# Final norm with tokens on partitions behind the eighth expert, and router logits from the un-normalised stream

## The chip, the core and the metric

The kernel runs on one core of one Trainium2 chip. The core has engines that run side by side and meet at semaphores: TensorE (PE, with PEld for its weight loads), VectorE (DVE), ScalarE (ACT), GpSimd (POOL) and SyncE (SP), which here issues every DMA. Each engine has a sequencer that works through its own list of instructions, branches included. The metric is the device time of one execution in microseconds (us); lower is better. A profiled execution also has a span, from the first to the last record of the program.

## The reference

A trunk of two layers over 256 tokens of 1024 features. Each layer adds a gated mixer, a cross-attention and a channel mixer to the stream h. In layer 1 the channel mixer is a mixture of 8 experts, of which each token takes two, and a norm ends the whole:

```python
def rms_norm(x, g):
    x32 = x.astype(jnp.float32)
    y = x32 * lax.rsqrt(jnp.mean(x32 * x32, axis=-1, keepdims=True) + EPS)
    return (y * g.astype(jnp.float32)).astype(x.dtype)

def moe_swiglu(xn, router_w, w1, w3, w2):
    ...
    logits = (xt @ router_w).astype(jnp.float32)
    top_v, top_e = lax.top_k(logits, TOP_K)
    gate = jax.nn.softmax(top_v, axis=-1)
    ...
    def expert_block(args):
        xblk, e = args
        return (jax.nn.silu(xblk @ w1[e]) * (xblk @ w3[e])) @ w2[e]
    ...

        hn = rms_norm(h, norm_ffn_g[l])
        ...
            h = h + moe_swiglu(hn, router_w[j], moe_w1[j], moe_w3[j], moe_w2[j])
    return rms_norm(h, final_norm_g)
```

The second choice's logit less the first's decides the gates; the order of a token's logits does not change when all of them are multiplied by the token's 1/rms.

## The kernel before

**Layout.** The stream `h` lies with features on partitions: 8 blocks of 128 features by 256 tokens (`h[:, k, :]`). Weights come from HBM in chunks of 1 MB (`raw`, 128x2048). For each chunk ACT writes a rounded copy `w_hi`, DVE the rest `w_lo`, and PE forms each product from three fp32r matmuls (`three`, L1519 to L1521), so that it keeps fp32's accuracy. Each engine's list is written out by hand; nothing reorders it. ACT and DVE split a chunk three steps ahead of the one whose results they post-process.

**Layer 1 up to the experts.** The last four chunks are the attention's output projection (`xo`, chunks `XO0` to `XO0 + 3`, 48 matmuls each). Behind each, DVE adds the result to a quarter of the stream (`residual`, L1143) and signals `h_att`; ACT squares that quarter into `cacc` (`square`, L673), and PE sums the squares over features with a matrix of ones (`sum_squares`, L1566), two chunks later. When all four are summed, ACT takes the root (L677), DVE the reciprocal (L1033), then DVE multiplies the stream by the gain and 1/rms into `xf` (L1040), while ACT and DVE split `xf` into `b_hi` and `b_lo`. From `xf` PE forms the 8 logits of each token (L1802, 16 fp32 matmuls) and turns it so that tokens lie on partitions (`by_token`, L1810); ACT copies that to `h_tok`. DVE finds each token's two experts (`route`, L1435 to L1459), with an exponential on ACT (L988) for the gates, and PE counts ranks within experts (L1819). `select` (L1374) makes a 0/1 matrix of the tokens of an expert, and the gather (L1829) multiplies `h_tok` by it. DVE then keeps books of further blocks (`further_blocks`, L1464 to L1486), which exist when an expert has more than 128 tokens.

**The experts.** A loop of 8 passes (L1919 for PE, `e_block`) has 42 chunks in each. At the end of a pass ACT and DVE write the expert's gated result to `y_hi_e` and `y_lo_e` (L973, L1416), tokens' slots on partitions. Within the next pass PE spreads it back to the tokens (`spread_out`, L1901 and L1902) and DVE adds it to `h` (L1389). The gather for the next expert also stands in the pass (L1913).

**The end.** Each engine then reads the number of blocks (`value_load`, L1922 for PE, L554 for SP) and runs a second loop of 3 passes (L1923, L555), each under an `If` (L1924, L556) around a whole further block. Then PE, ACT and DVE drain and meet at `settled`. Only now is the last expert spread and added to `h` (L1506), squared (L1003), summed (L1933), its root taken (L1005), the reciprocal formed (L1508), the norm applied (L1510) and turned (L1810), copied by ACT (L1008) and stored in two DMAs (L560).

## Time and profile before

| | us |
|---|---|
| median of 3 runs | 2162.11 |
| lowest, highest | 2160.7, 2167.48 |
| profiled execution | 2162.14 |
| its span | 2160.3 |
| PE busy | 2059.6 |
| DVE busy | 1637.2 |
| ACT busy | 1299.9 |

A timeline row tells when an instruction (or a run of like ones, with x and their number) started, how long it took, its engine, line, operation and tiles, and in brackets how long its engine had been idle and what ended that. An fp32 matmul stands as two records, an fp32r matmul or a transpose as one. Engines with a q (PEldq, SPq) are the sequencers. A window row has for each engine the busy time and the number of instructions, then the granted clock of PE as a share of full speed and the DMA's share.

### The profile page before, as it was taken

Reading aid. Unit: us, or ns where it says so; the run is one execution under the profiler, and the core shown is the slowest. Engines: PE = TensorE matmul, PEld = TensorE weight load, DVE = VectorE, ACT = ScalarE, POOL = GpSimd, SP = SyncE. Lnnn points to the kernel's source line nnn. Section 1 sums busy time; section 2 is a strip of 40 time slices with the busy share of each in tenths; the row PEclk is TensorE's granted clock in tenths of the full one; section 3 lists DMA queues with packets and bytes.
Section 4 is the critical chain, followed back from the end, with each engine's and each line's share of the span. In section 5 each row is a group of like instructions: output and inputs, shape, how many; then the busy total and the mean of one; then the engine's idle time right before and its main releaser. Section 6 shows DMA issues by size and latency. Waiting matters only on the chain.

```text
span 2160.3 us, 33554 instructions
## 1 busy us (share of the span) xinstructions
PE 2059.6 (95%) x12929; PEld 1871.5 (87%) x12929; DVE 1637.2 (76%) x1704; ACT 1299.9 (60%) x1133; POOL 13.2 (1%) x71
## 2 busy tenths in 40 slices
PE   8998999999998998989979999999999999999996
PEld 8988989889998988989878888888888888888885
DVE  6988656554446888656559888888988888898885
ACT  6664354343334664454337777777777777777774
POOL 0000000000000000000000000000000000000000
PEclk9998999999999999999989999999999999999998
DMA  8544445435554545445437999999999999999892
GB/s 248 176 124 161 132 155 176 151 117 181 190 176 145 167 124 161 135 152 175 139 136 285 385 325 376 330 366 353 354 373 331 376 332 367 343 366 373 328 377 91
DMA packets 309518, 526.76 MB, mean 244 GB/s; under 512 B 13566, under 2 KB 156582, under 8 KB 309414
## 3 DMA queue, kind: packets, MB, share of 16 engines
q1 hardware_dynamic: 309414, 525.29, 69.7%
q8 instruction: 75, 1.23, 0.2%
q14 instruction: 29, 0.24, 0.0%
HBM read 524.21 MB, written 1.05 MB: 243 GB/s over the span
## 4 chain that ended last, share of the span: by engine, by line
PE 80%; DVE 9%; issue 4%; ACT 4%; SPq 1%; PEldq 0%; DMA 0%; PEld 0%; DVEq 0%; ACTq 0%; POOL 0%
PE ps L1519 25%; PE ps L1521 24%; PE ps L1520 24%; DVE w_lo L1017 2%; DVE c L1083 2%; ACT w_hi L662 2%; PE ps L1839 1%; ACT w_hi L669 1%; PE ps L1913 1%; PE ps L1634 1%; DVE cacc L1067 1%; PE ps L1566 1%; PE ps L1654 1%; PE ps L1901 0%; PE ps L1902 0%
## 5 line engine op out<-in xcount | busy, mean ns | idle before, releaser
L1017 DVE TENSOR_TENSOR w_lo<-raw,w_hi 128x2048 fp32r<-128x2048 f32 x330 | 752.5, 2281 | 368.4 <-ACT w_hi L662 304.4
L1519 PE MATMUL ps<-w_hi,a_hi 128*128 128x512 f32 (+1 forms) x1472 | 566.1, 385 | 0.6 <-DVE h L1389 0.4
L1521 PE MATMUL ps<-w_hi,a_lo 128*128 128x512 f32 (+1 forms) x1472 | 560.5, 381 | 0.0
L1520 PE MATMUL ps<-w_lo,a_hi 128*128 128x512 f32 (+1 forms) x1472 | 559.7, 380 | 0.0
L662 ACT ACTIVATE w_hi<-raw 128x2048 fp32r<-128x2048 f32 x159 | 301.4, 1896 | 292.0 <-PE ps L1521 284.2
L1519 PE MATMUL ps<-a_hi,w_hi 128*128 128x256 f32 x1520 | 442.2, 291 | 24.1 <-DVE a_lo L1017 16.2
L1520 PE MATMUL ps<-a_lo,w_hi 128*128 128x256 f32 x1520 | 436.6, 287 | 0.0
L1521 PE MATMUL ps<-a_hi,w_lo 128*128 128x256 f32 x1520 | 436.1, 287 | 0.0
L669 ACT ACTIVATE w_hi<-raw 128x2048 fp32r<-128x2048 f32 x171 | 328.0, 1918 | 123.4 <-PE ps L1521 123.4
L1521 PEld LDWEIGHTS ps<-w_hi,a_lo 128*128 128x128 f32 x1472 | 276.5, 188 | 53.6
L1519 PEld LDWEIGHTS ps<-w_hi,a_hi 128*128 128x128 f32 x1472 | 276.7, 188 | 51.5 <-DVE w_lo L1017 0.8
L1519 PEld LDWEIGHTS ps<-a_hi,w_hi 128*128 128x128 f32 x1520 | 298.5, 196 | 26.3 <-issue 17.8
L1520 PEld LDWEIGHTS ps<-w_lo,a_hi 128*128 128x128 f32 x1472 | 276.8, 188 | 50.6
L1520 PEld LDWEIGHTS ps<-a_lo,w_hi 128*128 128x128 f32 x1520 | 298.4, 196 | 0.5
L1521 PEld LDWEIGHTS ps<-a_hi,w_lo 128*128 128x128 f32 x1520 | 298.0, 196 | 0.0
L1519 PE MATMUL ps<-b_hi,w_hi 128*128 128x256 f32 x744 | 214.3, 288 | 15.8 <-DVE b_lo L1017 14.7
L1521 PE MATMUL ps<-b_hi,w_lo 128*128 128x256 f32 x744 | 212.3, 285 | 0.0
L1520 PE MATMUL ps<-b_lo,w_hi 128*128 128x256 f32 x744 | 212.3, 285 | 0.0
L1519 PEld LDWEIGHTS ps<-b_hi,w_hi 128*128 128x128 f32 x744 | 144.6, 194 | 17.6 <-DVE b_lo L1017 10.7
L1017 DVE TENSOR_TENSOR w_lo<-mem_t,w_hi 128x2048 fp32r<-128x2048 f32 x56 | 128.4, 2292 | 21.7 <-ACT w_hi L669 21.6
L1520 PEld LDWEIGHTS ps<-b_lo,w_hi 128*128 128x128 f32 x744 | 144.6, 194 | 0.2
L1521 PEld LDWEIGHTS ps<-b_hi,w_lo 128*128 128x128 f32 x744 | 144.6, 194 | 0.0
(284 smaller groups left out, 2169.9 us busy)
## 6 DMA issues: line engine op xcount, KB each, us to landing
raw<-in_moe_w SPq DMA_DIRECT2D x171, 1024.0 KB, 6.6
raw<-in_w_in SPq DMA_DIRECT2D x68, 1024.0 KB, 5.2
mem_t<-in_moe_w SPq DMA_DIRECT2D x56, 1024.0 KB, 6.4
area<-in_moe_w SPq DMA_DIRECT2D x56, 1024.0 KB, 6.3
xf<-in_moe_w SPq DMA_DIRECT2D x56, 1024.0 KB, 6.0
raw<-in_ffn_w SPq DMA_DIRECT2D x33, 1024.0 KB, 5.3
raw<-in_w_mlstm_out SPq DMA_DIRECT2D x8, 1024.0 KB, 5.0
raw<-in_w_out SPq DMA_DIRECT2D x8, 1024.0 KB, 5.0
```

What stands on the lines that cost most here:

```text
L662: act.activation(w_hi[c % SPL][:, 0:n], raw[c % RAW][:, 0:n], ACT.Copy).then_inc(hi_done.sem, 1)
L669: act.activation(w_hi[m % SPL][:, :], e_raw[m % ERAW][:, 0:CH], ACT.Copy).then_inc(e_hi.sem, 1)
L1017: return dve.tensor_tensor(dst, whole, as_f32(hi), ALU.subtract)
L1067: ins = dve.scalar_tensor_tensor(dst, src, tap, dst, ALU.mult, ALU.add)
L1083: ins = dve.scalar_tensor_tensor(dst, src, tap, dst, ALU.mult, ALU.add)
L1519: pe.matmul(dst, wh, xh, start=start, stop=False, skip_group_check=True)
L1520: pe.matmul(dst, wh, xl, start=False, stop=False, skip_group_check=True)
L1521: return pe.matmul(dst, wl, xh, start=False, stop=stop, skip_group_check=True)
L1566: ins = pe.matmul(ps[4][:, 0:T], ones[:, :], sq[:, j % 2, i * T:(i + 1) * T], start=(j == 0 and i == 0), stop=(j == 3 and i == 1), skip_gr ...
L1634: ins = pe.matmul(ps[4 + hd % 2][:, tt * T:(tt + 1) * T], q_t[:, k, tt * P:(tt + 1) * P], k_t[:, k, :], start=(tt == 0 and e == 0), stop=( ...
L1654: ins = pe.matmul(ps[7][:, e * T:(e + 1) * T], vx[:, m, hd, e * P:(e + 1) * P], z_sig[:, 4 + 2 * (hd % 2) + m, :], start=(e == 0 and m == ...
L1839: ins = pe.transpose(ps[6][:, k * P:(k + 1) * P], act_e[g % 2][:, k * P:(k + 1) * P], ident[:, :])
```

## The change

**The logits.** The weights of the router are loaded behind the load of chunk `WO0` and multiplied by the norm's gain on DVE (8 instructions behind chunk `XK0`). In layer 1 `router_pair` takes the place of `sum_squares` for the last norm, one chunk behind the addition and no longer two: it forms logits from `h` itself (4 matmuls) and sums the squares for tokens on partitions (4 matmuls with one column of ones). ACT writes `xf = h * gain` by pairs behind its squares. The norm on features (`norm(layer, 2, ...)`) is made in layer 0 only. 1/rms is a column of one number per token, `r_stat[1]`; it scales `h_tok` in ACT's copy, and the difference of the two best logits. The order of `route` changes: ranks and `select(0)` stand ahead of the gates, which get a semaphore of their own (`gate_ready`). The three zeroing instructions (`sel_t`, `y_hi_e`, `y_lo_e`) move from the start of `route` to the first `xo` step. The split of chunk 2 of the first expert moves behind the routing on ACT and behind `gather_lo(0)` on DVE. `further_blocks` works on tables that lie side by side, with three instructions in a row where it had seven each.

**The final norm.** `tail(b)` stands on PE, ACT and DVE directly behind the loop of 8, ahead of the loop over further blocks (and inside its `If`, for a further block). PE turns `h` into four banks by products with the identity and adds the last expert's result into the same banks, with tokens on partitions. ACT squares the banks with a sum along the row; DVE and ACT form 1/rms as a column; DVE multiplies the banks by it and by the final gain, which is broadcast to `vb_pool` early. SP stores four tiles of 128x512 (`store`) ahead of its own loop over further blocks. `settled` goes.

```diff
+            def router_pair(layer, n, j):
+                if j == 0:
+                    pe.wait_ge(rw_scaled, KB)
+                pe.wait_ge(h_att.sem, h_att.at(layer, j + 1))
+                for k in (2 * j, 2 * j + 1):
+                    for tt in range(TT):
+                        ins = pe.matmul(ps[5][:, tt * NE:(tt + 1) * NE], h[:, k, tt * P:(tt + 1) * P], rw[:, k, :],
+                                        start=(k == 0 and tt == 0), stop=(k == KB - 1), skip_group_check=True)
+                if j == 3:
+                    ins.then_inc(logits_mul, 1)
...
-                    if c >= XO0 + 2:
-                        sum_squares(layer, 2, c - XO0 - 2)
-                for j in (2, 3):
-                    sum_squares(layer, 2, j)
+                    if c > XO0:
+                        (router_pair if layer else sum_squares)(layer, 2, c - XO0 - 1)
+                (router_pair if layer else sum_squares)(layer, 2, 3)
...
+                if layer and j == XO0:
+                    multiplied(layer, j)
+                    ch.did(dve.tensor_scalar(sel_t, h[:, 0, :], 0.0, None, ALU.mult))
+                    ch.did(dve.tensor_scalar(y_hi_e, flat2(h)[:, 0:D], 0.0, None, ALU.mult))
+                    ch.link(dve.tensor_scalar(y_lo_e, flat2(h)[:, 0:D], 0.0, None, ALU.mult))
                 if XO0 <= j < N_MIX:
                     residual(layer, j, j - XO0, h_att)
...
+                    if layer and j == XO0:
+                        act.activation(warm, eps[:, 0:1], ACT.Sqrt)
                     act.wait_ge(h_att.sem, h_att.at(layer, j - XO0 + 1))
                     square(layer, 2, j - XO0)
+                    if layer:
+                        for k in (2 * (j - XO0), 2 * (j - XO0) + 1):
+                            ins = act.activation(xf[:, k, :], h[:, k, :], ACT.Copy, scale=col(0, R_NORM + 16 + k))
+                        ins.then_inc(xg_done, 1)
...
+            def tail(b):
+                act.activation(warm, eps[:, 0:1], ACT.Sqrt)
+                for n in range(2):
+                    for tt in range(TT):
+                        i = 2 * n + tt
+                        act.wait_ge(f_mul.sem, f_mul.at(b, i + 1))
+                        act.activation(f_junk[i], ps[2 * tt + n][:, :], ACT.Square, accum_out=f_stat[0][:, i:i + 1]).then_inc(f_sq.sem, 1)
...
+            def tail(b):
+                for tt in range(TT):
+                    for j in range(KB):
+                        pe.matmul(ps[2 * tt + j // 4][:, (j % 4) * P:(j % 4 + 1) * P], h[:, j, tt * P:(tt + 1) * P], ident[:, :],
+                                  start=(j % 4 == 0), stop=False, skip_group_check=True)
+                for n in range(2):
+                    pe.wait_ge(y_lo_done.sem, y_lo_done.at(b, n + 1))
...
             with pe.Fori(0, NE) as b:
                 e_block(b)
+            tail(NE - 1)
             pe.wait_ge(ids_done, 1)
             more = pe.value_load(ids[0:1, NBLK + 1:NBLK + 2], min_val=NE, max_val=NBLK)
             with pe.Fori(NE, NBLK) as b:
                 with pe.If(b < more):
+                    pe.wait_ge(f_out.sem, f_out.at(b, 0))
                     e_block(b)
-            pe.drain().then_inc(settled, 1)
-
-            pe.wait_ge(settled, 3)
-            spread_out(f_spread)
...
+                    tail(b)
```

On PE, from the end of the last projection to the gather, before (in `cacc` lie squares, in `wif` the router's weights, in `u_pad` masks, in `q_t` `h_tok`):

```order
L1521 MATMUL ps<-a_hi,w_lo 128x256
L1566 MATMUL ps<-cacc,ones 128x256 x6
L1802 MATMUL ps<-wif,xf 128x8 x16
L1810 MATMUL ps<-ident,xf 128x128 x16
L1819 MATMUL ps<-u_pad,k_t 128x8
L1819 MATMUL ps<-u_pad,ones 128x8
L1819 MATMUL ps<-u_pad,k_t 128x8
L1819 MATMUL ps<-u_pad,ones 128x8 x2
L1829 MATMUL ps<-vx,q_t 128x128 x16
```

And in the change:

```order
L1577 MATMUL ps<-a_hi,w_lo 128x256
L1632 MATMUL ps<-wif,h 128x8 x4
L1640 MATMUL ps<-ones,cacc 128x1 x4
L1632 MATMUL ps<-wif,h 128x8 x4
L1640 MATMUL ps<-ones,cacc 128x1 x4
L1877 MATMUL ps<-ident,xf 128x128 x16
L1886 MATMUL ps<-u_pad,k_t 128x8
```

The 16 logits are in groups of four now, each with four sums; two such groups stand further up, behind the second and the third of the last four chunks, where the third had a sum of 2 matmuls.

On DVE, at the last `xo` steps of layer 1, before:

```order
L1017 TENSOR_TENSOR w_lo<-raw,w_hi 128x2048
L1143 TENSOR_TENSOR h<-h,ps 128x512 x2
L1017 TENSOR_TENSOR w_lo<-raw,w_hi 128x2048
L1143 TENSOR_TENSOR h<-h,ps 128x512
L1017 TENSOR_TENSOR w_lo<-raw,w_hi 128x2048
L1143 TENSOR_TENSOR h<-h,ps 128x512
L1033 RECIPROCAL rstd<-rstd 128x256
```

And in the change:

```order
L1054 TENSOR_TENSOR w_lo<-raw,w_hi 128x2048
L1314 TENSOR_SCALAR b_hi<-h 128x256
L1315 TENSOR_SCALAR b_hi<-h 128x1024
L1316 TENSOR_SCALAR b_lo<-h 128x1024
L1180 TENSOR_TENSOR h<-h,ps 128x512 x2
L1054 TENSOR_TENSOR w_lo<-raw,w_hi 128x2048
L1180 TENSOR_TENSOR h<-h,ps 128x512
L1054 TENSOR_TENSOR w_lo<-raw,w_hi 128x2048
L1180 TENSOR_TENSOR h<-h,ps 128x512
L1490 TENSOR_REDUCE u_pad<-ps 128x1 x2
```

Three zeroing instructions stand ahead of the first addition, and the choice of experts follows the last one directly.

On PE, behind the last expert matmul, before (the first row is inside the `If` of the loop over further blocks):

```order
L1521 MATMUL ps<-w_hi,a_lo 128x512
L1924 UNCONDITIONAL_BRANCH
L1923 REGISTER_ALU
L1923 COMPARE_AND_BRANCH
L1901 MATMUL ps<-b_hi 128x256
L1902 MATMUL ps<-b_hi,b_lo 128x256
...
L1933 MATMUL ps<-cacc,ones 128x256 x8
L1810 MATMUL ps<-ident,xf 128x128 x16
```

And in the change, behind the loop of 8:

```order
L2000 COMPARE_AND_BRANCH
L1990 MATMUL ps<-ident,h 128x128 x16
L1997 MATMUL ps<-b_hi 128x512
L1998 MATMUL ps<-b_lo,b_hi 128x512
...
L2004 TENSOR_LOAD ids
L2004 ISA x2
L2005 UNCONDITIONAL_BRANCH
L2006 COMPARE_AND_BRANCH
```

The spreading (8 matmuls of 512 columns) and the turning now stand ahead of the loop over further blocks; nothing but branches stands behind it.

## Rows read from the trace of the kernel before

**Rows 1.** The page, section 1: busy time, share of the span and instructions.

```profile
PE 2059.6 (95%) x12929; PEld 1871.5 (87%) x12929; DVE 1637.2 (76%) x1704; ACT 1299.9 (60%) x1133; POOL 13.2 (1%) x71
```

**Rows 2.** Timeline of PE, from the last projection to the second group.

```profile
1094.74 1.02 PE L1566 MATMUL ps<-cacc,ones 128*128 128x256 f32 x4
1095.41 0.47 PE L1519 MATMUL ps<-a_hi,w_hi 128*128 128x256 f32 x1
...
1101.35 2.93 PE L1566 MATMUL ps<-cacc,ones 128*128 128x256 f32 x12
1111.22 7.00 PE L1802 MATMUL ps<-wif,xf 128*128 128x8 f32 x32 [6.94 <-DVE xf L1040]
...
1123.14 0.59 PE L1819 MATMUL ps<-u_pad,ones 128*128 128x8 f32 x4
1127.24 5.96 PE L1829 MATMUL ps<-vx,q_t 128*128 128x128 f32 x32 [3.51 <-DVE k_t L1375]
1132.95 0.48 PE L1519 MATMUL ps<-w_hi,a_hi 128*128 128x512 f32 x1
...
1147.50 0.50 PE L1519 MATMUL ps<-w_hi,a_hi 128*128 128x512 f32 x1 [0.37 <-DVE h L1389]
```

**Rows 3.** Windows: PE, PEld, DVE, ACT, POOL busy, PEclk, DMA share, GB/s.

```profile
1111.20:1118.00 6.80, 6.78 (x32) 6.78 (x33) 4.96 (x6) 2.43 (x2) 0.00 (x0) 0.50 0.00 0
...
1127.20:1133.00 5.80, 5.76 (x33) 5.79 (x33) 0.69 (x1) 0.60 (x1) 0.00 (x0) 0.61 1.05 394
```

**Rows 4.** Timeline of DVE: last additions, zeroing, choice of experts, bookkeeping.

```profile
1087.64 0.68 DVE L1143 TENSOR_TENSOR h<-h,ps 128x512 f32<-128x512 f32 x1
1089.18 0.69 DVE L1143 TENSOR_TENSOR h<-h,ps 128x512 f32<-128x512 f32 x1 [0.86 <-PE ps L1521]
...
1116.07 0.69 DVE L1490 TENSOR_SCALAR b_hi<-h 128x1024 fp32r<-128x1024 f32 x1
...
1118.33 0.24 DVE L1435 COPY u_pad<-ps 128x8 f32<-128x8 f32 x2 [0.97 <-PE ps L1802]
...
1122.16 0.23 DVE L1447 TENSOR_TENSOR u_pad<-u_pad 128x8 f32<-128x8 f32 x2
...
1134.47 0.15 DVE L1464 COPY u_pad<-ps 128x8 f32<-128x8 f32 x1
...
1140.95 0.16 DVE L1486 CAST ids<-u_pad 1x16 int32<-1x16 f32 x1
```

**Rows 5.** Timeline of ACT, at the exponential of the gates.

```profile
1122.33 1.28 ACT L988 ACT_TABLE_LOAD   x1
```

**Rows 6.** Timelines of ACT, DVE and PE, from the eighth expert's end.

```profile
2115.65 1.92 ACT L669 ACTIVATE w_hi<-xf 128x2048 fp32r<-128x2048 f32 x1 [0.80 <-PE ps L1521]
...
2118.61 4.08 PE L1913 MATMUL ps<-vx,q_t 128*128 128x128 f32 x32
...
2129.35 1.91 ACT L669 ACTIVATE w_hi<-raw 128x2048 fp32r<-128x2048 f32 x1
2129.76 1.40 DVE L1416 SCALAR_TENSOR_TENSOR b_lo<-ps,k_t,b_hi 128x512 fp32r<-128x512 f32 x2
...
2138.36 0.58 PE L1901 MATMUL ps<-b_hi 128*128 128x256 f32 x1 [10.21 <-PEq L1926]
...
2140.41 0.63 ACT L1003 ACTIVATE cacc<-h 128x512 f32<-128x512 f32 x1 [9.15 <-DVE h L1506]
```

**Rows 7.** Single lines: duration ns min/median/max, first and last start us, or landing.

```profile
L1919 PEldq COMPARE_BRANCH  x8: 76/208/233, 1254.4 to 2124.0; - x8
...
L1922 PEldq TENSOR_LOAD <-ids x1: 490/490/490, 2124.2 to 2124.2; - x1
...
L1924 PEldq COMPARE_BRANCH  x3: 221/3829/7295, 2125.2 to 2137.8; - x3
...
L554 SPq TENSOR_LOAD <-ids x1: 278/278/278, 2112.0 to 2112.0; - x1
...
L555 SPq COMPARE_BRANCH  x3: 40/45/54, 2117.6 to 2119.0; - x3
...
DMA to landing us min/median/max: 2.7/3.1/3.6
```

More of the change, by code:

```diff
@@ L272, in trunk @@
         x_stat, m_stat = ([small[:, f + 2 * i:f + 2 * i + 2] for i in range(3)] for f in (48, 54))
+        f_stat = [small[:, f:f + n] for f, n in ((52, 4), (56, 2), (58, 2), (60, 2))]
+        f_junk = [vflat[:, T + i * 512:T + (i + 1) * 512] for i in range(3)] + [flat2(z_sig)[:, D:D + 512]]
+        f_tile = (flat2(cacc), flat2(c31))
+        r_stat = [small[:, 48 + 2 * i:50 + 2 * i] for i in range(2)]
         def table(n):
@@ L557, in _ @@
                     expert_block(b, sp.value_load(ids[0:1, bass.ds(b, 1)], min_val=0, max_val=NE - 1))
-            sp.wait_ge(out_ready, 4)
-            for t in range(TT):
-                sp.dma_start(out[0, t * P:(t + 1) * P, :], q_t[:, 4 * t:4 * t + 4, :].rearrange("p k n -> p (k n)")).then_inc(out_sem, 16)
-            sp.wait_ge(out_sem, 32)
+                    store(b)
+                    sp.wait_ge(out_sem, 64 * b - 64 * (NE - 2))
+                    sp.sem_inc(free, 1)
+            sp.wait_ge(out_sem, 64)
         @block.gpsimd
@@ L914, in mixer @@
                         ahead(layer, c - N_MIX)
-                std(layer, 2)
-                norm_hi(layer, 2, b_hi)
-                ahead(layer, SPL - 1)
+                if layer == 0:
+                    std(layer, 2)
+                    norm_hi(layer, 2, b_hi)
+                    ahead(layer, SPL - 1)
+                else:
+                    act.wait_ge(summed.sem, summed.at(layer, 12))
+                    act.activation(r_stat[0], ps[4][:, 0:TT], ACT.Sqrt, bias=eps[:, 0:1], scale=1.0 / D).then_inc(r_std, 1)
+                    act.activation(warm, eps[:, 0:1], ACT.Exp)
             def dense(layer):
@@ L1338, in mixer @@
                         ahead(layer, c - N_MIX)
-                norm(layer, 2, R_NORM + 16, b_hi, b_lo)
-                ahead(layer, SPL - 1)
+                if layer == 0:
+                    norm(layer, 2, R_NORM + 16, b_hi, b_lo)
+                    ahead(layer, SPL - 1)
             def dense(layer):
@@ L1443, in route @@
                     if top is best:
[L1444 to L1445 removed]
+                        dve.wait_ge(r_std, 1)
+                        dve.reciprocal(r_stat[1], r_stat[0]).then_inc(r_rst, 1)
+                        both(lambda tt, c: dve.scalar_tensor_tensor(logit[tt], one[tt], -3e38, raw_logit[tt], ALU.mult, ALU.add))
                 for tt in range(TT):
@@ new lines, in further_blocks @@
+                ch.link(ins)
+                for j in range(N_OVER):
+                    one = over_oh[j].rearrange("p (a b) -> p a b", a=1).broadcast_to([P, 1 + 3 * TT, NE])
+                    ins = dve.tensor_tensor(prods[j], by_expert, one, ALU.mult)
+                ch.link(ins)
+                for j in range(N_OVER):
+                    ins = dve.tensor_reduce(by_block[:, :, NE + j:NE + j + 1], prods[j], AX, ALU.add)
+                ch.link(ins)
+                r = by_block[:, 1:1 + TT, NE:NE + N_OVER]
@@ L1796, in _ @@
                     dense(layer)
-            pe.wait_ge(xf_done.sem, xf_done.moe)
-            pe.wait_ge(rw_in, 16)
-            for tt in range(TT):
-                for k in range(KB):
-                    ins = pe.matmul(ps[5][:, tt * NE:(tt + 1) * NE], xf[:, k, tt * P:(tt + 1) * P], rw[:, k, :],
-                                    start=(tt == 0 and k == 0), stop=(k == KB - 1), skip_group_check=True)
-            ins.then_inc(logits_mul, 1)
+            pe.wait_ge(xg_done, 4)
             def by_token(done):
@@ L1924, in _ @@
                 with pe.If(b < more):
+                    pe.wait_ge(f_out.sem, f_out.at(b, 0))
                     e_block(b)
-            pe.drain().then_inc(settled, 1)
-            pe.wait_ge(settled, 3)
-            spread_out(f_spread)
-            for j in range(4):
-                pe.wait_ge(f_sq, j + 1)
-                for i in range(2):
-                    ins = pe.matmul(ps[4][:, 0:T], ones[:, :], sq[:, j % 2, i * T:(i + 1) * T], start=(j == 0 and i == 0), stop=(j == 3 and i == 1),
-                                    skip_group_check=True)
-                ins.then_inc(f_sum, 1)
-            pe.wait_ge(f_x, 2)
-            by_token(f_t)
+                    tail(b)
     return nc
```

181 lines of the change are left out of this document (102 added, 79 removed).

## The prediction, made before the changed kernel ran

> **What bounds the kernel now.** The page first: PE is busy 95% of the span [rows 1], so only stretches in which PE does not multiply, or does what it need not, have anything to give. The timeline of PE shows two around this change. The front one runs from 1101.35 us (last projection of layer 1 over) to 1132.95 us (first expert matmul) [rows 2]. In it a serial chain decides: squares, root, reciprocal, normalised stream, 7.00 us of logits, top-2 choice on DVE, ranks, gather. PE idled 6.94 us ahead of the logits; the windows say that it then worked at the lower of its two clock levels (0.50, 1.2 GHz), and at 0.61 in the gather [rows 3]. The back one runs from 2128.2 us (last expert matmul over: 2138.36 less 10.21) to 2160.3 us. There PE waits 10.21 us for its own sequencer [rows 6]: the three passes of the loop over further blocks, all jumped over, took it from 2124.2 us to the end of that wait, with branches of up to 7.3 us [rows 7]. Only then do spreading, squares, norm, transposes and stores begin. Between the two, eight experts take 124.2 us each (the loop's branch, eight times from 1254.4 to 2124.0 [rows 7]), 42 chunks of 2.72 us (1.92 of ACT's split and its 0.80 of waiting for PE [rows 6]) and some 10 us of small work, with PE never waiting for long; the change adds one semaphore per expert there that DVE sets a whole expert ahead: nothing.
>
> **Front: what is lost in the projections.** In layer 1 the last four chunks (the output projection of attention) used to have one 2-matmul sum of squares among them, 0.67 us from its start to the next chunk [rows 2]. Now a pair is 8 fp32 matmuls of 8 columns or 1. The nearest rows: 16 logits in 7.00 us at the half clock, 0.22 each at the full one, and the five rank matmuls, which were over at 1123.73, 1.34 us behind the masks, 0.26 each [rows 2, 4]; I take 0.23, so 1.85 us a pair. Pair 0 goes between the second and the third of these chunks, pair 1 before the fourth, where the sum stood. Pair 0 also waits: its half of the stream was there at 1088.32 us (row 1087.64) but three zeroing instructions now stand ahead of that addition on DVE, a small one and two of 0.69, 1.5 us in all [rows 4], so it is there at 1089.8 us, while the second chunk ends at 1089.1 us (it released the row of 1089.18). PE waits 1.0 us with the semaphores. Sum: 1.0 + 1.85 + (1.85 - 0.67) = 4.0 us; bounds 2.5 (no wait, 0.20 each) and 6 (ACT's squares behind its added table load and copies hold two pairs). The last chunk ends at 1105.35 us.
>
> **Front: what is taken off the chain.** Pair 2 needs no wait (1.85 us), the logits of pair 3 follow (0.9): logits complete at 1108.1 us, not at 1118.2. The square root, the reciprocal, the eight normalising products and the splits into b_hi and b_lo leave the chain: nothing reads b_hi and b_lo of this norm. DVE's choice took from 1118.33 to 1122.39 us [rows 4]; less the copy out of PSUM (0.27), plus a reciprocal of two columns (0.1): 3.9 us, masks at 1112.1. Ranks, 1.3 with the semaphore: 1113.4. Then DVE copies ranks and one table and selects, five small instructions more or less like the pair of 0.24 [rows 4], 1.4 us with their semaphores, where it waited for ACT's exponential (1.28 us of table load, [rows 5]) and did the gates first: gather at 1114.9 instead of 1127.24. **12.3 us.** What could be later: h_tok. Transposes (DVE no longer feeds them, ACT's scaled copies xf do) start behind pair 3 at 1109.0 and last 2 to 3.6 us; ACT takes the root at 1109.1, loads a table (1.28) and copies four tiles in 2.5: 1113.3, 1.6 us ahead of the gather. The split of chunk 2 that ACT does next (1.9) ends at 1115.5, before the first half of the gather. On SP, the loads of chunks 5 to 7 wait for these transposes alone and leave some 11 us sooner.
> The gather took 5.96 us [rows 2] at 0.61 clock; at full clock the row of 4.08 us is the same work [rows 6]. Before it PE will have had gaps of about 1 and 1.5 us, not 6.94: I take 5.0, **1.0 us** more.
> Behind the start of the experts the first matmul of the second group stood at 1147.50, 14.55 us after the first expert matmul, though four chunks of 2.72, the 1.9 of spreading (16 matmuls of 256 columns) and 0.7 of small work are 13.5. It waited for DVE, whose bookkeeping of further blocks ran from 1134.47 to 1141.1, 6.6 us [rows 2, 4]. It is now some 3 us in wider instructions, though with the split of chunk 2 ahead of it; the wait should go: **0.8 us**; bounds 0 and 1. Front: 12.3 + 1.0 + 0.8 = 14.1 us.
>
> **Back.** PE now turns the stream and spreads the last expert in one accumulation into four banks, directly behind the last expert matmul: 16 fp32 matmuls at 0.235 (4.08 us for 16 with a small wait inside) to 2132.0, then 8 of 512 columns at 0.227 (a twelfth of a chunk), to 2133.9; the last y_lo is there at 2131.16 [rows 6] and hides. ACT is done with its look-ahead split at 2131.26, loads the root's table (1.28) and starts squaring at 2132.8; four squares with their sums at 0.68 (the 0.63 of the squares of before [rows 6] and, an estimate, 0.05 for the read of the sum) end at 2135.5. Sum, root, reciprocal on columns of two, 0.7 in all; four products out of PSUM on DVE at 0.65: 2138.8; the fourth store is issued at 2139.3 and lands, by 3.1 us [rows 7], at 2142.4.
> That is not the end. The jumping loop now lies **behind** the tail on each engine. PE can start it when the last matmuls are handed over, about 2131.4, and by its 14.1 us is through at 2145.5. SP went from 2112.0 to 2119.0 through the same loop, 7.1 us [rows 7]; that was hidden, since it waited long for the output anyway; it now starts after the fourth issue: 2146.4. DVE and ACT begin theirs earlier than SP; by SP's 7.1 us DVE too is through by 2146. With 0.5 for the closing it ends at 2146.9 instead of 2160.3: **13.4 us**. Bounds: 17.5, where the landing ends it, and 6, where a branch has one more fetch.
> One rule bears on this. The Trainium skill, "Runtime: NRT & Kernel Launch", section "Instruction fetch mechanics", says that a taken branch to a target outside the window of fetched pages stalls for a DMA, and that fetching ahead is otherwise sequential. The trace agrees: one branch of PE's took 7.3 us, the shortest of the same line 0.2 [rows 7].
>
> **Other edits with no price.** The scaling of the router's weights (8 instructions of about 0.15 in a stretch where DVE waits for ACT) and the final gain's broadcast (512 KB, once, behind a chunk load with two more chunks in hand) are covered by PE's projections. If that cover is gone, they cost their own 1 and 4 us. Layer 0's sum of squares one chunk earlier is within 0.2.
>
> **Rivals.** *Jumps hidden* (for it: of PE's three equal branches the shortest took 0.2 us, and SP now stands some 24 us ahead of its loop with nothing to do; against: PE stands only 7 us, and its second jump was the longest): if all branches are like the shortest, the loops take some 2 us, and the store's landing ends the program, 4 us better, 2130.6. The skill's page of above says that fetching ahead goes on sequentially, which would favour this one. *One more fetch* (the loop body is longer by the tail on each engine; PE's second branch cost 7.3): on PE 2145.5 + 7.3, ending 6 to 7 us later: 2141. *The projections pay more* (ACT has a table load, squares and two copies per pair in the order of its splits; gather at the half clock): 6 us of the front go: 2140.6. *Slower*: the choice is now made on raw sums; if one expert gets more than its 128 slots where it had fewer, a ninth block of 124.2 us runs with a second tail: 2259 us. It decides at 129 tokens in one expert; mean load is 64, and before all three further passes were jumped over. The same count of blocks would come from any ordering of the same logits, so it needs logits that differ in more than rounding. *It does not do what it says*: if the tail still waits for the jumps (a wait that holds PE until the loop is through), only the cheaper norm counts, about 5 of the 13: 2143.
>
> **How the numbers follow.** The profiled run took 2162.14 us for a span of 2160.3, the median of the runs is 2162.11: no correction. 2162.1 - 14.1 - 13.4 = **2134.6 us**. Chances: forecast 0.60, jumps hidden 0.15, one more fetch 0.11, projections pay more 0.08, tail not early 0.02, ninth block or another loss 0.02, and 0.02 for gains eaten up by something that I do not see. The range 2129 to 2144 takes in the forecast with its bounds, the hidden jumps and the two on the upper side: about 0.9, less what I may have overlooked. A measurement of this kernel tells 0.3%, 6.5 us, from no change. Faster 0.96, same 0.02, slower 0.02.
>
> **What would show it.** Right: first expert matmul near 1118 to 1121 us; fp32 matmuls of 8 columns with waits of about 1 us at the first pair only; last projection 4 us later; no gap of 10 us behind the last expert matmul; the fourth store issued near 2125 us (2139.3 less the front's 14.1); then 5 to 8 us with nothing but branches of SP and PE. Wrong: long waits of PE at each pair, an expert period other than 124.2 us, PE waiting for DVE or a DMA in the first expert, or stores that are held up by ACT. The weakest terms are the jumps (4 us down, 7 up) and the clock in the gather.

## The result and the profile after

The changed kernel ran in 2142.97 us (median of four runs, 2135.98 to 2144.22), the kernel before beside it in 2162.9. The ratio is 0.9899, 95% interval 0.9884 to 0.9915. The profiled execution took 2144.22 us, its span is 2142.5. The forecast was 2134.6, with a range of 2129 to 2144: the time lies inside, 1.0 us below its upper end and 8.4 us above the forecast (the profiled execution lies 0.2 us beyond that end), and the gain is 19.9 us (17.8 between the two profiled spans) where 27.5 were expected.

Page of the changed kernel, section 1; it answers [rows 1].

```profile
PE 2058.8 (96%) x12937; PEld 1872.8 (87%) x12937; DVE 1622.2 (76%) x1646; ACT 1298.2 (61%) x1140; POOL 19.4 (1%) x65
```

The front, as the timeline of PE shows it in the changed kernel; it answers [rows 2]. L1632 are the logits, L1640 the column sums of squares, L1877 the transposes, L1886 the ranks, L1896 the gather, L1575 projection and expert.

```profile
1098.03 1.03 PE L1632 MATMUL ps<-wif,h 128*128 128x8 f32 x8 [0.86 <-DVE h L1180]
1098.92 1.03 PE L1640 MATMUL ps<-ones,cacc 128*128 128x1 f32 x8
...
1107.13 0.96 PE L1632 MATMUL ps<-wif,h 128*128 128x8 f32 x8
1107.94 1.03 PE L1640 MATMUL ps<-ones,cacc 128*128 128x1 f32 x8
1108.84 0.36 PE L1575 MATMUL ps<-a_hi,w_hi 128*128 128x256 f32 x1
...
1114.67 0.96 PE L1632 MATMUL ps<-wif,h 128*128 128x8 f32 x8
...
1117.56 1.85 PE L1640 MATMUL ps<-ones,cacc 128*128 128x1 f32 x8
1119.27 3.65 PE L1877 MATMUL ps<-ident,xf 128*128 128x128 f32 x16
1122.72 0.43 PE L1886 MATMUL ps<-u_pad,k_t 128*128 128x8 f32 x2
...
1126.15 5.94 PE L1896 MATMUL ps<-vx,q_t 128*128 128x128 f32 x32 [1.29 <-DVE vx L1421]
1131.85 0.48 PE L1575 MATMUL ps<-w_hi,a_hi 128*128 128x512 f32 x1
```

From the end of the projections to the first expert matmul it is now 1114.67 to 1131.85, 17.2 us, where it was 31.6 (1101.35 to 1132.95): the chain did become 14.4 us shorter. But the projections end 13.3 us later than before, so the experts start only 1.1 us earlier. The windows (columns as in [rows 3]) say where TensorE's clock was at its lower level:

```profile
465.10:471.80 6.70, 5.89 (x27) 5.92 (x28) 5.50 (x10) 3.69 (x4) 0.00 (x0) 0.50 0.00 0
666.50:673.20 6.70, 4.12 (x19) 4.15 (x20) 5.88 (x13) 3.93 (x5) 0.00 (x0) 0.50 0.01 2
1079.50:1086.20 6.70, 4.86 (x15) 4.17 (x16) 3.08 (x5) 0.98 (x2) 0.00 (x0) 0.50 0.48 157
...
1099.90:1103.30 3.40, 3.40 (x18) 3.40 (x18) 0.80 (x1) 2.56 (x3) 0.00 (x0) 0.50 1.05 396
1117.00:1130.60 13.60, 12.31 (x59) 12.24 (x59) 6.24 (x43) 6.67 (x11) 0.00 (x0) 0.50 0.48 167
```

In the kernel before the first two of these places show the lower clock for half as long, and the third and the output projection not at all (its windows, same columns):

```profile
462.70:466.10 3.40, 3.40 (x19) 3.40 (x17) 3.04 (x6) 2.25 (x3) 0.00 (x0) 0.51 0.00 0
466.20:472.00 5.80, 5.80 (x51) 5.80 (x51) 2.37 (x2) 2.72 (x3) 0.00 (x0) 1.00 0.24 61
664.10:667.50 3.40, 3.04 (x14) 3.07 (x15) 3.31 (x8) 1.88 (x4) 0.00 (x0) 0.50 0.02 5
...
1073.00:1077.20 4.20, 1.52 (x7) 1.40 (x8) 3.22 (x4) 0.63 (x1) 0.00 (x0) 1.00 0.37 105
1077.30:1101.30 24.00, 24.00 (x198) 23.87 (x197) 10.23 (x8) 8.05 (x7) 0.00 (x0) 1.00 0.44 156
```

The back, in the timelines of ACT, DVE and PE of the changed kernel; it answers [rows 6].

```profile
2125.81 3.73 PE L1990 MATMUL ps<-ident,h 128*128 128x128 f32 x32
...
2129.09 1.28 ACT L1028 ACT_TABLE_LOAD   x1
2130.39 0.20 ACT L1028 ACTIVATE u_pad<-eps 128x1 f32<-128x1 f32 x1
2130.50 0.58 ACT L1033 ACTIVATE vx<-ps 128x512 f32<-128x512 f32 x1
...
2133.72 1.41 DVE L1555 SCALAR_TENSOR_TENSOR cacc<-ps,small,vb_pool 128x512 f32<-128x512 f32 x2
2135.05 1.40 DVE L1555 SCALAR_TENSOR_TENSOR c<-ps,small,vb_pool 128x512 f32<-128x512 f32 x2
```

And the single lines of branches and stores (columns as in [rows 7]); L2006 is PE's, L579 and L578 are SyncE's passes over the jumped loop, L572 the stores.

```profile
L2006 PEldq COMPARE_BRANCH  x3: 221/221/3646, 2130.1 to 2135.1; - x3
...
L579 SPq COMPARE_BRANCH  x3: 50/50/55, 2138.3 to 2141.7; - x3
...
L578 SPq COMPARE_BRANCH  x3: 40/45/54, 2140.7 to 2142.0; - x3
...
L572 SPq DMA_DIRECT2D out<-c x2: 427/428/430, 2135.9 to 2136.5; - x2
...
DMA to landing us min/median/max: 2.5/2.8/3.3
```

The gap of 10.21 us is gone; transposes follow the last expert matmul at once, the fourth store is issued at 2136.5, lands at 2139.8 (3.3 us later), and SyncE ends its loop at 2142.0. Of PE's branches one took 3.6 us; before, one took 3.8 and one 7.3.

All profiles can be laid side by side with five marks of the PE timeline: first matmul of layer 1's output projection, its last, the first and the last matmul of the experts, the end. Each stretch runs from the start of one mark to the start of the next. In the last column is how long the clock was at its lower level before the first mark.

| kernel | projection begins | projection | to first expert | experts | back | lower clock before |
|---|---|---|---|---|---|---|
| before | 1077.3 | 23.9 | 31.7 | 994.8 | 32.5 | 58.0 |
| changed | 1084.5 | 30.0 | 17.3 | 993.7 | 16.9 | 73.4 |
| after_again | 1083.6 | 30.0 | 17.3 | 993.8 | 17.5 | 70.0 |
| tail_only | 1077.8 | 24.0 | 31.7 | 994.8 | 16.9 | 58.0 |
| tail_only_again | 1079.3 | 24.7 | 32.3 | 994.8 | 17.2 | 56.3 |
| router_only | 1084.5 | 30.1 | 17.3 | 993.7 | 29.6 | 69.9 |
| no_further | 1081.3 | 30.1 | 17.3 | 993.7 | 13.4 | 63.1 |
| logits_behind | 1084.1 | 28.9 | 18.1 | 993.8 | 17.4 | 73.3 |
| fill | 1081.8 | 30.1 | 17.2 | 993.8 | 17.3 | 63.0 |
| zero_behind | 1082.0 | 27.5 | 15.8 | 993.7 | 17.5 | 69.9 |
| l0_back | 1078.3 | 27.8 | 17.3 | 993.8 | 16.9 | 61.4 |
| both_mended | 1080.9 | 27.4 | 15.7 | 993.7 | 17.0 | 59.8 |
| one_jump | 1080.5 | 27.4 | 15.7 | 993.7 | 15.3 | 59.8 |
| l0_early_only | 1082.5 | 24.7 | 32.3 | 994.8 | 29.3 | 69.9 |

### The profile page after: what moved, and what is told of

Same layout as the page of the kernel before. It is cut to its first block, busy times and chain, and to the rows that moved or that the text cites. A ratio compares the mean times of both kernels' runs of the same rounds, so it can differ in the third digit from the quotient of the medians.

```text
span 2142.5 us, 33505 instructions
## 1 busy us (share of the span) xinstructions
PE 2058.8 (96%) x12937; PEld 1872.8 (87%) x12937; DVE 1622.2 (76%) x1646; ACT 1298.2 (61%) x1140; POOL 19.4 (1%) x65
## 4 chain that ended last, share of the span: by engine, by line
PE 81%; DVE 8%; issue 4%; ACT 4%; SPq 1%; DMA 0%; POOL 0%; DVEq 0%; ACTq 0%
PE ps L1575 25%; PE ps L1577 25%; PE ps L1576 25%; DVE w_lo L1054 2%; ACT w_hi L684 2%; DVE c L1120 2%; PE ps L1906 1%; ACT w_hi L691 1%; PE ps L1981 1%; PE ps L1728 1%; PE ps L1708 1%; DVE cacc L1104 1%; PE ps L1622 1%; DMA raw<-in_w_in 0%; DVE xf L1138 0%
## 5 line engine op out<-in xcount | busy, mean ns | idle before, releaser
L1575 PE MATMUL ps<-w_hi,a_hi 128*128 128x512 f32 (+1 forms) x1472 | 565.9, 384 | 0.0
L1575 PE MATMUL ps<-a_hi,w_hi 128*128 128x256 f32 x1520 | 443.9, 292 | 25.3 <-DVE a_lo L1054 17.5
L1575 PEld LDWEIGHTS ps<-a_hi,w_hi 128*128 128x128 f32 x1520 | 299.8, 197 | 27.8 <-issue 18.0
L1575 PEld LDWEIGHTS ps<-w_hi,a_hi 128*128 128x128 f32 x1472 | 276.8, 188 | 50.2
L1575 PE MATMUL ps<-b_hi,w_hi 128*128 128x256 f32 x744 | 214.9, 289 | 15.1 <-DVE b_lo L1054 14.7
L1575 PEld LDWEIGHTS ps<-b_hi,w_hi 128*128 128x128 f32 x744 | 145.1, 195 | 16.8 <-DVE b_lo L1054 10.7
```

Of the source, the lines that this page charges most:

```text
L1575: pe.matmul(dst, wh, xh, start=start, stop=False, skip_group_check=True)
```

## Experiments: which part is worth what

The theory behind them: the chain and the tail do what was forecast, and what is missing is time at the lower clock ahead of and inside the output projection. Rivals: that this slip is chance (P) or brought by the change (C); for the back, that the loop or the landing decides.

**after_again**: the changed kernel once more, no edit.

> The changed kernel, unchanged, once more. In its first profile it was 8.0 us behind the kernel before already ahead of the output projection of layer 1's attention (split 158 of VectorE), where the two kernels differ by next to nothing, and it had 17 us more at half clock up to there; half of that is 8.5 us. Theory P (position): where the half-clock stretches fall is chance from run to run. Then this profile shows another slip there, anything from -3 to 10 us, equal to half of the extra half-clock time, and the runs spread over 8 to 10 us as in the first four (2136 to 2144), with a median of 2138 to 2142. Rival C (caused): the earlier sums of squares in layer 0 and the moved loads put the stretches there. Then the slip is 8 us again with the same stretches within 3.4 us, and the median is 2143 to 2144.

Measured: 2143.47 us (2141.72 to 2144.03, five runs), ratio 0.991 [0.9897, 0.9924]. The projection began at 1083.6 with 70.0 us of lower clock before it, against 1084.5 and 73.4. That speaks for C: the slip comes back to within 1 us, and of nine runs of this kernel eight lie at 2141.7 or above.

**tail_only** and **tail_only_again**: the kernel before with the new final norm.

```
+            tail(NE - 1)
...
-            spread_out(f_spread)
...
-            by_token(f_t)
```

> The kernel before with the final norm of the changed one alone (and its load of the final gain; the router's path is that of before). From the last expert matmul to the end the changed kernel took 16.5 us, before 32.1. Theory: the back part is independent of the front and worth 15.6 us: 2146.5 us if before gives 2162.1. The prediction's sum would give 13.4 (2148.7), with PE's passes over the jumped loop at 14.1 us; the theory wants them at 6 to 8 us. Under rival C (the slip ahead of the output projection comes with the front part) this kernel has no slip there; under P it has one between -5 and 9 us.

> The kernel before with the final norm of the changed one alone, once more. Its profiled run took 2146.9 us, 15.2 less than the profiled run of before and by the 15.6 read from the trace, but the median of its runs was 2151.2, with a clock of 0.978 where the profiled run had 0.980. If the difference is half-clock stretches in the layers ahead (theory), a profile of a run of 2150 or more shows the back stretch at 16.9 us again and the output projection of layer 1 beginning 3 to 5 us later than 1077.8; a profile of a run near 2147 shows neither. Rival: the back stretch itself varies, 16.9 to 21 us.

Measured: 2151.24 us (2146.89 to 2151.62) and 2149.77 (2146.79 to 2151.1), ratios 0.9947 [0.9933, 0.996] and 0.9933 [0.9918, 0.9947]. The back takes 16.9 and 17.2 us, so the rival that it varies by itself falls. The second profile, of a run of 2150.05 us, is 3.2 us longer between its ends: 1.5 of it before the projection, 0.8 in it, 0.6 behind it, 0.3 at the end. That is less than the theory wanted at the first place, and the 1.5 us there are not more time at the lower clock in total (56.3 us against 58.0), so of the theory only the two stretches behind hold (1.8 and 3.4 us more of the lower clock); where the 1.5 us come from stays open. Against their neighbours' runs the tail alone gives 11.5 and 13.7 us, on average 12.6 and not 15.6.

**router_only**: the kernel before with everything but the final norm.

```
+                        (router_pair if layer else sum_squares)(layer, 2, c - XO0 - 1)
...
 spread_out(f_spread)
```

> The kernel before with the router's change alone (logits from the un-normalised stream, sums of squares one chunk earlier in both layers, zeroing moved, bookkeeping in wide instructions); the final norm is that of before, behind the jumped loop. In the profile of the changed kernel the stretch from the last projection to the first expert matmul took 17.2 us instead of 31.6 (-14.4), the four last projection chunks took 5.3 us more, 1.7 of it by a half-clock stretch. Theory P: -14.4 + 3.6 and -1 in the first expert, -9 to -12: 2150 to 2153 us. Rival C: the slip of 8 us belongs to this part, so 2158 to 2161, no difference that can be told. The branches of PE behind the eighth expert should take about 14 us as in before.

Measured: 2156.32 us (2152.07 to 2157.06), ratio 0.9967 [0.9955, 0.9979]: a gain of 6.4 us, between the two theories' numbers and nearer to C, with the slip in the profile (1084.5). And its back took 29.6 us, not 32.5, though the final norm is that of before. Its line of PE's branches against [rows 7]:

```profile
L1976 PEldq COMPARE_BRANCH  x3: 221/221/3686, 2123.0 to 2128.0; - x3
```

The branch of 7.3 us, on which the prediction built 14.1 us, occurs in one profile of the thirteen that have this loop or one jump over it, that of before. From 2120 to 2145 us the queue of instruction transfers moved six packets there and two here (before, then router_only; packets, MB, share), so in before more code was fetched behind the eighth expert; why is open.

```profile
q8 instruction: 6, 0.10, 2.1%
```

```profile
q8 instruction: 2, 0.03, 0.7%
```

Where the old norm stands and it is missing, the back is 29.3 and 29.6 us, and 29.4 - 16.9 = 12.5 us is what the tail is worth; the medians say 12.6.

**no_further**: the loop over further blocks left out, on all engines.

```
-            with sp.Fori(NE, NBLK) as b:
-                with sp.If(b < more):
...
```

> The changed kernel with the loop over further blocks left out on all four engines (for these data all its passes are jumped over, so the output is the same; it leaves out the work that other data would need). In the changed kernel SyncE went through it in 5.1 us behind the fourth store's issue (2136.9 to 2142.25 us). Theory: what is then left is the landing of that store, by the 3.1 us of before's, so the end is at 2140.0 + 0.3: 2.0 us less than the changed kernel. Rival: the store lands within the loop long before its end, and all 5 us go. A third: nothing goes, since the closing of the other engines sets the end.

Measured: 2137.68 us (2137.44 to 2139.97), ratio 0.989 [0.9875, 0.9905]; back 13.4, 3.5 us less than in the changed kernel, between theory and rival. The stores, by the line of no_further:

```profile
L572 SPq DMA_DIRECT2D out<-c x2: 332/332/333, 2132.6 to 2133.2; - x2
...
DMA to landing us min/median/max: 2.1/2.1/2.1
```

From the fourth issue to the end it is 2.5 us, where the changed kernel needs 6.0. The store lands sooner than in the changed kernel (2.1 instead of up to 3.3 us); instruction transfers stand beside it there (six packets on their queue q14 from 2120 us on, one here), but that they slow it is not shown.

## Experiments: where the front's gain went

**l0_back**: layer 0's sums of squares two chunks behind, as before; layer 1 as changed.

```
-                    if c > XO0:
-                        (router_pair if layer else sum_squares)(layer, 2, c - XO0 - 1)
+                    if layer and c > XO0:
+                        router_pair(layer, 2, c - XO0 - 1)
+                    if layer == 0 and c >= XO0 + 2:
+                        sum_squares(layer, 2, c - XO0 - 2)
```

> The changed kernel with layer 0's sums of squares at the place of before (two chunks behind; layer 1 as changed). In four profiles of kernels with the router's change the first output-projection chunk of layer 1 began at 1084.5, 1083.6, 1084.5 and 1081.3 us, in the two without it at 1077.3 and 1077.8; less half of the half-clock time up to there all six are 1047.8 to 1049.7. Theory C (caused, by layer 0's sums, which now make TensorE wait and drop the clock at the end of layer 0): this kernel begins that chunk at 1077 to 1079 us and the median falls by 3 to 6 us to 2138 to 2140. Theory P (where a wait of 4 us of TensorE meets the clock's stretches is a matter of position, not of this edit): 1081 to 1085 us as the four, or anything from 1077, and a median of 2141 to 2144.

Measured: 2135.31 us (2134.7 to 2137.77), ratio 0.9875 [0.9853, 0.9896], below the whole interval of after_again. C holds, and by more than expected: 8.2 us between the medians. In the profiles 6.2 us of it lie ahead of the output projection (1078.3 for 1084.5) and 2.2 in it: it lasts 27.8 us, not 30.0, with no lower clock (window of l0_back), though PE's wait of 0.86 us is still there.

```profile
1078.30:1106.10 27.80, 26.94 (x226) 26.73 (x224) 11.64 (x11) 11.82 (x15) 0.00 (x0) 1.00 0.37 135
```

This is 3.9 us more than before, and the prediction had 4.0.

The timeline of PE shows what the edit does at the end of layer 0. Changed kernel, then l0_back; L1622 are the sums of squares:

```profile
458.34 1.02 PE L1622 MATMUL ps<-cacc,ones 128*128 128x256 f32 x4
459.94 1.13 PE L1622 MATMUL ps<-cacc,ones 128*128 128x256 f32 x4 [0.58 <-ACT cacc L695]
465.91 0.55 PE L1575 MATMUL ps<-b_hi,w_hi 128*128 128x256 f32 x1 [4.84 <-DVE b_lo L1054]
```

```profile
455.67 2.93 PE L1622 MATMUL ps<-cacc,ones 128*128 128x256 f32 x12
463.44 0.36 PE L1575 MATMUL ps<-b_hi,w_hi 128*128 128x256 f32 x1 [4.85 <-DVE b_lo L1054]
```

Three sums behind the last chunk used to fill the time in which DVE adds and ACT squares the last quarter. One of them now stands ahead of that chunk and delays it by 0.67 us, and PE idles 0.58 us in its place. That is 0.5 us, against the 0.2 predicted. What follows is larger: the clock is low for 6.8 us from 465.0, not 3.4, and again at 666.4 (6.8, not 3.4) and at 1079.4 (6.8, none before). Each extra 3.4 us at half clock costs 1.7 where PE is busy.

**l0_early_only**: that one edit on the kernel before.

```
+                    if layer == 0 and c > XO0:
+                        sum_squares(layer, 2, c - XO0 - 1)
+                    if layer and c >= XO0 + 2:
+                        sum_squares(layer, 2, c - XO0 - 2)
```

> The kernel before with one edit of the change alone: in layer 0 each sum of squares one chunk earlier (layer 1 as before). The prediction priced it at 0.2 us at most. Theory C, from the kernel with this undone (output projection of layer 1 begins at 1078.3 instead of 1081 to 1084.5 us, 8 us faster): it begins at 1082 to 1085 instead of 1077.3, and the median is 4 to 8 us above that of before, 2167 to 2171. Rival: on the kernel before the later half-clock stretches fall otherwise, and only the 0.7 us of the sum ahead of the last chunk and 1.7 us of clock at the end of layer 0 remain: +2.4, 2165. A third: nothing, 2162.5, if the effect needs the other edits.

Measured: 2166.54 us (2162.08 to 2168.92, twelve runs) against 2163.5, ratio 1.0013 [1.0004, 1.0021]. A loss of 3.0 us, less than C wanted and near the rival's 2.4. Between the two profiles it is 6.6 us up to the last expert matmul, of which the back, without the branch of 7.3 us, returns 3.2. The profile begins the projection at 1082.5 and has the window of the changed kernel:

```profile
1077.50:1084.20 6.70, 4.87 (x15) 4.16 (x16) 3.07 (x5) 0.99 (x2) 0.00 (x0) 0.50 0.47 157
```

Over all fourteen profiles: with layer 0's sums as before the projection begins at 1077.3 to 1080.9 us (six, mean 1079.0), with the earlier sums at 1081.3 to 1084.5 (eight, mean 1083.0). The groups lie 0.4 us apart at the nearest. They part clearly if the time is taken from a mark ahead of the edit: from the 2,501st record of the three-product matmuls (370.7 to 372.9 us in all profiles) to the projection it is 706.2 to 708.1 us in the six and 710.6 to 711.6 in the eight. In this stretch the clock is low for 32.4 to 35.9 us in the six and 45.9 to 49.5 in the eight. So the edit costs some 4 us up to the projection; around it up to 3 us are chance, since kernels with the same code up to there differ by as much.

**zero_behind**: the zeroing behind the first residual.

```
                 if XO0 <= j < N_MIX:
                     residual(layer, j, j - XO0, h_att)
+                if layer and j == XO0:
...
```

> The changed kernel with the three zeroing instructions of VectorE put behind the first residual of the output projection, not ahead of it. Theory: TensorE's wait of 0.9 us at the first router pair goes, and the stretch of the four output-projection chunks falls from 30.0 to 29.1 us; if that wait was what dropped the clock there (3.4 us at half clock in all four kernels with the router's change), to 27.4. Behind it nothing changes: 17.3 us to the first expert matmul. Rival: the squares that ScalarE does behind its copies hold the pair instead, and 30.0 stays. The time follows where the stretches of the layers before fall, 2139 to 2143.

Measured: 2138.82 us (2137.09 to 2141.03), ratio 0.989 [0.9869, 0.9912]. The wait of 0.86 us is gone, and the projection takes 27.5 us as the theory's second number said. That the wait was what dropped the clock does not follow: l0_back kept the wait and had no lower clock there. The 1.8 us of it that are left here reach in from before the projection. Unexpected: from the projections to the first expert matmul it is 15.8, not 17.3. PE's timeline in zero_behind:

```profile
1109.61 0.96 PE L1632 MATMUL ps<-wif,h 128*128 128x8 f32 x8
...
1113.10 1.94 PE L1877 MATMUL ps<-ident,xf 128*128 128x128 f32 x16
1116.30 0.39 PE L1886 MATMUL ps<-u_pad,k_t 128*128 128x8 f32 x2 [1.26 <-DVE u_pad L1501]
...
1118.87 6.63 PE L1896 MATMUL ps<-vx,q_t 128*128 128x128 f32 x32 [1.29 <-DVE vx L1421]
```

At the upper clock the transposes take 1.94 us, not 3.65, and the gather starts 9.3 us behind the projections, not 11.5. The prediction had 9.55 (1105.35 to 1114.9). The gather itself is slower here, 6.4 us to the first expert matmul for 5.7, because the lower clock now falls on it (0.50 from 1118.0 to 1124.7).

**logits_behind**: all logit matmuls behind the last chunk.

```
+                if j == 3:
+                    for i in range(4):
+                        router_logits(layer, i)
```

> The changed kernel with the 16 logit matmuls all behind the last projection chunk; the column sums of squares stay between the chunks. Theory (the pairs cost what their matmuls last, 0.83 us for four logits): output projection 30.0 - 0.9 (wait) - 1.7 (two pairs of logits) = 27.4 us, less 1.7 if its half-clock stretch goes too; from the last projection to the first expert matmul 17.3 + 1.7 = 19.0. Sum 1 to 2.6 us better than the changed kernel. Rival (clock): a longer run of narrow matmuls behind the projections brings the lower clock sooner or for longer, each logit at 0.22 to 0.44 us, and the second stretch is 20.5 to 22: no gain or a loss of 1 to 2.

Measured: 2142.98 us (2139.77 to 2144.09), ratio 0.9903 [0.9881, 0.9925]: no difference. Projection 28.9, then 18.1 us, together 0.3 less than in the changed kernel. The matmuls move from one stretch to the other at their own price, and the wait ahead of the first pair does not go but grows, from 0.86 to 1.43 us: it is the squares that PE now waits for. That the later stretch would pay for it in clock did not show (its lower-clock time was 10.2 us, not 13.7), nor did the gain of 1 to 2.6.

**fill**: six wide matmuls, whose result is not used, ahead of the last pair.

```
+                if j == 3:
+                    for i in range(6):
+                        pe.matmul(ps[5][:, T:2 * T], ones[:, :], h[:, 0, :], start=False, stop=False, skip_group_check=True)
```

> The changed kernel with six more matmuls of ones by 256 columns of the stream (as wide as those of the old sums of squares, 0.24 us each; their result is not used) ahead of the last pair. In all kernels with the router's change the clock is at its lower level for 13.7 us from some 2 us behind the last projection, and transposes (3.65 us), ranks (2.1) and gather (5.9) run at it. Theory (the clock follows how wide TensorE's work is, and the eight narrow matmuls of a pair are as good as idling): the fill keeps the upper level past the transposes; it costs 1.5 us and gives back 2 to 4: stretch 17.3 to 14.8 to 16.8 us. Rival (the clock falls whatever is put there): 18.8 us and a time 1.5 us longer.

Measured: 2142.21 us (2138.78 to 2143.23), ratio 0.9901 [0.9879, 0.9924]. The fill itself took 2.67 us, not 1.5 (12 records of 0.22 in the trace: each of these matmuls is two records, and the expectation had counted one). The stretch is 17.2 us with that in it, and its windows show the upper clock up to the gather:

```profile
1111.90:1124.60 12.70, 10.16 (x80) 9.56 (x79) 6.12 (x38) 7.38 (x12) 0.00 (x0) 1.00 0.26 88
1124.70:1128.00 3.30, 3.30 (x18) 3.30 (x17) 1.09 (x6) 0.60 (x1) 0.00 (x0) 0.50 1.05 397
```

The fill paid for itself and no more. It is no proof of the theory: zero_behind kept the upper clock through the same pairs and transposes without any fill. Narrow matmuls are therefore not enough to lose it; what decides between the two is left open.

**both_mended** and **one_jump**: l0_back and zero_behind together; then also one condition around the loop on each engine.

```
+            with sp.If(more > NE):
+                with sp.Fori(NE, NBLK) as b:
```

> The changed kernel with two edits of the last round together: layer 0's sums of squares two chunks behind as in before, and VectorE's zeroing behind the first residual. Alone they gave 2135.3 and 2138.8 us (medians) against 2143.3. Theory (they act at different places): output projection begins at 1078.3, lasts 27.76 less the wait of 0.9, 26.9 us; then 15.8 to 17.3 us to the first expert matmul, depending on whether the clock is low for 6.8 or 13.7 us there; 993.8; 16.9. Sum 2132 to 2134 of span, 2134 to 2136 as time. Rival (position decides: another start of the output projection brings other half-clock stretches, whatever the edits): 2137 to 2143.

> both_mended, with the loop over further blocks put inside one more condition on each engine, so that with no further block it is jumped over once, not entered and jumped over three times. With the loop left out, the end came 2.2 us behind the issue of the fourth store; in the changed kernel SyncE needed 5.1 us for the loop behind that issue. Theory: one jump costs SyncE about what its longest did, 2.3 us, and the landing of 2.2 us then decides as much: 2.5 to 3.1 us less than both_mended. Rival (the cost is fetching the code behind the loop, paid once, however many jumps): less than 1 us.

Measured: 2135.87 us (2135.04 to 2137.74), ratio 0.9872 [0.9858, 0.9886], and 2134.56 (2132.41 to 2134.77), ratio 0.9862 [0.9848, 0.9877]. The two front edits don't add: projection and stretch behind it are the shortest of all kernels with the router's change (27.4 and 15.7), but the projection began at 1080.9 where l0_back had 1078.3, with the same code up to there. That is the chance of above, and four runs each can't part the two. Against zero_behind, from which both_mended differs by the edit in layer 0 alone, it is 3.0 us between the medians, where the same edit gave 8.2 without the zeroing moved. one_jump has the lowest median of all kernels, 8.9 us below the changed kernel's 2143.47; from l0_back and both_mended its interval does not part it. Its single jump still takes SyncE from 2129.7 to 2132.3:

```profile
L578 SPq COMPARE_BRANCH  x1: 50/50/50, 2129.7 to 2129.7; - x1
```

```profile
L186 SPq COMPARE_BRANCH  x1: 38/38/38, 2132.3 to 2132.3; - x1
```

In the changed kernel the first jump took 2.3 us (2138.3 to 2140.6) and the other two 0.7 each. So most of the price is in the first jump, paid once; the back is 1.7 us shorter, between the theory's 2.5 to 3.1 and the rival's less than 1.

## Why the prediction was right, and where it was off

The forecast case held in its main lines: the chain behind the projections is shorter, the tail stands ahead of the jumps, and SyncE's way through the loop ends the program. Of the rivals none happened as a whole; nearest came *the projections pay more*, whose 6 us and whose gather at the lower clock are in the trace, though not from ACT's work. The sum came out 9.7 us too high (27.5 against 17.8 between the spans). That the time still fell into the range is in part luck: of the front's 14.1 us the two profiles show 2.2 and the medians 6.4, and the back gave 2.2 us more than forecast between the profiles. Of the signs named, the wait at the first pair alone, the closed gap, the expert period of 124.2 us and the last 5.6 us of branches were right; the first expert matmul at 1131.85 us (forecast: 1118 to 1121) and the fourth store at 2136.5 (forecast: 2125) were not. Step by step:

- **Up to the output projection: 0 predicted, 7.2 us lost** (1077.3 to 1084.5). This is the step that failed: "Layer 0's sum of squares one chunk earlier is within 0.2." Of the 7.2 us, 1.8 arose ahead of that edit (at the mark of 371 us) and are chance, 5.4 behind it. Its own delay is 0.5 us; with the clock it is 4.0 on average (eight profiles against six). The table says that it is clock: 15.4 us more at half speed, worth 7.7.
- **In the projections: 4.0 predicted, 6.1 lost.** The wait was 0.86 (1.0), the pairs 1.78 and 1.71 (1.85), so 3.7 at the upper clock. Time at the lower clock, which the forecast did not have there, added the rest: 5.1 us, of which 1.7 reach in from before the projection. In l0_back, without it, the term was 3.9, so the working was right; moving the zeroing took the wait and the later 3.4 us of lower clock away.
- **Behind them: 17.3 predicted (12.3 and 4.0 and 1.0), 14.4 gained.** The order of events was right to 0.3 us at the upper clock (zero_behind: 9.3 for 9.55). In the changed kernel transposes and ranks ran at the lower one, and 4.5 of the gather's 5.9 us: the forecast had looked for PE's gaps alone, and PE did not idle before the clock fell, it was in narrow matmuls. Of the gather's 1.0 us nothing came (5.70 us from its start to the first expert matmul, 5.71 before).
- **In the first expert: 0.8 predicted, 1.1 gained**; DVE's bookkeeping took 2.8 us (1135.56 to 1138.39) for 6.6.
- **Back: 13.4 predicted, 15.6 between the two profiles, 12.5 between usual runs.** From the last expert matmul to the fourth store it took 10.9 us to the end of its issue, and 11.1 were forecast (2128.2 to 2139.3). SyncE's loop was 5.1 us, not 7.1 (its first jump took 2.3 us, in before 4.8). PE's 14.1 us was one profile's slow branch read as a rule; it came to 6.6, and nothing hung on it, because SyncE was later.

By the Trainium skill, "Runtime: NRT & Kernel Launch", section "Instruction fetch mechanics", a jump outside the fetched pages waits for a fetch. The traces agree in place of the prediction's count of branches: one long first jump (SyncE 2.3 us, PE 3.6 in the changed kernel; 2.6 and 3.8 in one_jump), short ones behind it. It is not so on every engine: VectorE's first jump in the changed kernel took 0.6 us.

The medians tell it more steadily than the one pair of profiles: tail 12.6, router's part 6.4, together 19.0, and the whole change 19.3 (2162.73 to 2143.47). Of the router's part about 3 to 8 us were eaten by one edit in the other layer (medians: 3.0, 3.0 and 8.2; profiles: 4.0).

## What to carry to other kernels

Work of TensorE that stands behind the last projection of a stage may be what fills the wait for the other engines; pulled forward it saves nothing and turns into a wait, and an idle or a half-clock stretch there moves every later one. Price an edit that "only moves" a small matmul by the idle time that it leaves, at both levels of the clock. And take the length of a jump over unused code from several places or profiles: here PE's branch of the second pass was 7.3 us once and 0.2 us in all other profiles of such a loop.

## What the hardware showed beyond the expectation

The same wait of TensorE, 3.95 us for VectorE ahead of the output projection, left the clock alone in one kernel and halved it in another. Timeline of PE in the kernel before, then in the changed one:

```profile
1075.67 1.97 PE L1654 MATMUL ps<-z_sig,vx 128*128 128x256 f32 x8 [3.95 <-DVE xf L1162]
```

```profile
1081.34 3.75 PE L1728 MATMUL ps<-z_sig,vx 128*128 128x256 f32 x8 [3.95 <-DVE xf L1199]
```

The eight records behind it took 1.97 and 3.75 us. In the stretches shown here the lower clock came in or just behind waits of 4 to 7 us, once 1.9 us behind a wait of 0.86 us (1099.9 in the changed kernel; l0_back had the same wait and kept the upper clock), and in the changed kernel behind 2.3 us of matmuls with 8 columns or 1 with no wait. What decides is not shown. Up to the output projection, time less half of the lower-clock time was 1047.1 to 1051.1 us in all fourteen profiles, while the time itself went from 1077.3 to 1084.5: the clock explains much of the spread between runs, and up to 4 us remain beside it.
